# VectorE in place of GpSimd for the low parts of 24 weight units in the mixer of a one-core encoder block

## The chip, the cores and the metric

One core of a Trainium2 chip runs the whole kernel. The metric is the time of one execution on the device in microseconds. Engines are named as in the profile: PE is TensorE, DVE is VectorE, ACT is ScalarE, POOL is GpSimd, SP is SyncE.

## What is computed

One layer of a streaming encoder, on 512 tokens of width 1024, in float32:

```python
x = x + 0.5 * swiglu(rmsnorm(x, ffn1_norm), ffn1_w_gu, ffn1_w_down)
x = x + token_mixing(rmsnorm(x, mix_norm), w_in, lb, hg_norm, conv_w, conv_norm, w_out)
x = x + cross_attention(rmsnorm(x, xa_norm), rmsnorm(mem, mem_norm), xa_wq, xa_wkv, xa_wo)
x = x + 0.5 * swiglu(rmsnorm(x, ffn2_norm), ffn2_w_gu, ffn2_w_down)
return rmsnorm(x, final_norm)
```

`token_mixing` projects the normed x with one matrix (`w_in`, 1024 x 3584) to q, f, i (called v in the kernel) and g of a gated linear recurrence with 4 heads, and to B, C and u of a short convolution with 512 channels. The recurrence's state has a decay exp(cumsum(log f)); its output is normed and multiplied with silu(g). The convolution gives B * conv3(C * u), normed. Both halves together go through `w_out`.

## The kernel before, in words

**Products in three passes.** Every large product takes both of its operands apart into a high part (fp32r, a rounded copy) and a low part (the difference), and adds three matmuls: high x high, high x low, low x high. Lines L1642, L1643 and L1644 are these three.

**Weight units.** The weights lie in HBM as units of 128 x 1024 floats, in the order in which they are used. A unit goes through four steps in one of four slots of the buffers `raw`, `wh` and `wl` (`SLOTS = 4`): SP loads it into `raw` (L492); ACT makes the high part into `wh` (`hi`, L565, counted by the semaphore `hi_ready`); then the low part `wl = raw - wh` is made, counted by `lo_ready`; PE waits for `lo_ready` and multiplies (24 matmuls of 128x512 for a unit), and counts `unit_used`. ACT may make the high part of unit u + 4 only when unit u is used, so it does that in `ahead(u)`. SP reloads `raw` after `lo_ready` of the unit that lay there.

**Who makes the low part.** In parts of the two FFNs DVE does, in one instruction (`unit_low`, L1110). Everywhere else, the mixer included, GpSimd does, in four instructions of 128x256 (`lo`, L531, called from a loop over groups of four units, `whole`).

**The mixer.** The mixer's input projection uses 28 units, `U_MIX` to `U_WOUT` - 1, one in each of 28 slots of the program (the list `MIX_SLOTS`; these slots of time are not the four of the buffers). Slot `at` has a kind ("f", "q", "v", "g", "C", "u", "B") and a number of head or channel group. In slot `at`:
- PE multiplies unit `U_MIX + at` into one of four banks of PSUM (`bank`), after `group_read` says that DVE has read what was there four groups ago, and then does the matmuls of the head steps that the list `STEPS` puts there;
- DVE waits for the unit (`unit_used`), takes it out of the bank, and does its part of the head steps;
- ACT does its part, and `ahead(U_MIX + at)`: the high part of the unit four slots later. In ACT's order it stands behind the head steps O and L with a > 0 of the same slot, and ahead of the others.

The head steps are written out by hand. Head h begins in slot `HEAD_START[h]` = 1, 7, 12, 17 and takes a step in each slot: A (scan of the log decays), L0, L1, L2 (levels of the chunk's triangle), K, Q, S, O, N. In step L, DVE makes differences of b (L1352, L1353), ACT takes their exponentials (L818), DVE multiplies them with q and k (`factors`, L1362), PE makes scores of them (L1894) after the next unit, and DVE keeps the scores under a mask (L1372). L1 stands in slots 3, 9, 14 and 19, and its last DVE instructions are differences (of level 6). L2 stands in slots 4, 10, 15 and 20; in it DVE makes one more difference (L1410), and ACT takes two exponentials of it and of b (L837, L838). K (L1415) follows, then Q, with a transposition that DVE copies out (L1419), and S (L1429, L1431).

Slots 2 to 5 are the four units of v. They fill all four banks at once (four token tiles), and DVE takes them out in slot 5 with four instructions (L1521). PE's unit of slot 6, in the words of the prediction unit 6, uses the first of these banks again. `taps` (L1470 to L1475) makes a convolution after its u slot, and `normed` (L1442 to L1450) the output of a head. L1000 adds squares for a norm.

Of the kernel before, what the change touches and what calls it, by code (L numbers as in the profile page):

```python
# [34 lines left out]
SLOTS = 4  # L35
# [9 lines left out]
U_FFN1 = 0  # L45
# [3 lines left out]
U_MIX = U_DOWN1 + N_DOWN  # L49

MIX_SLOTS = [("f", 0), ("q", 0), ("v", 0), ("v", 1), ("v", 2), ("v", 3),
# [3 lines left out]
V_SLOT = MIX_SLOTS.index(("v", 3)) + 1  # L55
U_WOUT = U_MIX + len(MIX_SLOTS)
# [12 lines left out]
U_FFN2 = U_WO + KC  # L69
# [8 lines left out]
P_UNIT = 2 * NF  # L78
# [28 lines left out]
def block_kernel(nc, w_all, x_t, mem_t, params, consts_mask, ident_d, out):  # L107
    f32 = mybir.dt.float32
# [5 lines left out]
    MULT, ADD, SUB = ALU.mult, ALU.add, ALU.subtract  # L114

    ctx = ExitStack()
    with ctx:
        def sb(name, shape, dt=f32, where=ctx):
            return where.enter_context(nc.sbuf_tensor(name, shape, dt))

        def sem(name):
            return ctx.enter_context(nc.semaphore(name))


        raw = sb("raw", [128, SLOTS, UNIT])
        wh = sb("wh", [128, SLOTS, UNIT], f32r)
        wl = sb("wl", [128, SLOTS, UNIT], f32r)
# [83 lines left out]
        def by_chunk(ap):  # L211

            return ap.rearrange("p (g c t) -> p g c t", g=2, c=2)

        def mirrored(ap):

            *outer, (step, n) = [list(d) for d in ap.ap]
            return bass.AP(ap.tensor, ap.offset + step * (n - 1), outer + [[-step, n]])
# [108 lines left out]
        hi_ready = sem("hi_ready")  # L327
        lo_ready = sem("lo_ready")
# [197 lines left out]
        @block.gpsimd  # L526
        def _(pool):
            def lo(slot):
                for k in range(0, KC, 2):
                    two = slice(128 * k, 128 * k + 256)  # L530
                    ins = nc.gpsimd.tensor_tensor(wl[:, slot, two], raw[:, slot, two], wh[:, slot, two].bitcast(f32), SUB)  # L531
                ins.then_inc(lo_ready, 1)

            def whole(first, last):
                with pool.Fori(first // SLOTS, last // SLOTS) as i:
                    for c in range(SLOTS):
                        pool.wait_ge(hi_ready, i * SLOTS + (c + 1))
                        lo(c)

            def add_up(u0, which, j):  # L540

                p = j % 2
                u = u0 + 2 * (PRE[which] + j) + 1
                pool.wait_ge(raw_loaded[u % SLOTS], u // SLOTS * 16)
                pool.dma_start(raw[:, 2 * p + 1, :], w_all[u, :, :], accum_op=ADD).then_inc(up_added[p], 16)  # L545

            def pairs(u0, which):
                for j in range(ST[which]):
                    add_up(u0, which, j)
                pool.wait_ge(lo_ready, u0 + P_UNIT)  # L550

            pairs(U_FFN1, 0)
            whole(U_FFN1 + P_UNIT, U_FFN2 + SLOTS)
            pairs(U_FFN2, 1)
            whole(U_FFN2 + P_UNIT, NU)

# [394 lines left out]
        def _(dve):  # L951
            steps = [0]

            def link(ins):

                steps[0] += 1
                ins.then_inc(dve_step, 1)
                dve.wait_ge(dve_step, steps[0])
                return ins

            V_ = nc.vector
# [34 lines left out]
            def add_squares(n, off=0):  # L996
                dve.wait_ge(sq_ready, off + (n + 1))
                if n > 0:
                    dve.wait_ge(sq_added, off + n)
                V_.tensor_tensor(acc[:, :], acc[:, :], sq[:, n % 2, :], ADD).then_inc(sq_added, 1)  # L1000
# [9 lines left out]
            def clear():  # L1010

                cleared[0] += 1
                V_.memset(acc[:, :], 0.0).then_inc(acc_clear, 1)
                dve.wait_ge(acc_clear, cleared[0])
# [452 lines left out]
            def taps(at, c):  # L1467
# [6 lines left out]
                                             in1=convV, op0=MULT, op1=ADD))  # L1474
                link(V_.tensor_tensor(convV, convV, rstd[:, :], MULT))  # L1475

            rstd_twice = gbuf[:, 1, :]
            link(V_.tensor_tensor(rstd_twice, rstd[:, :], rstd[:, :], MULT))
            for at, (kind, c) in enumerate(MIX_SLOTS):
                g = SLOT_GROUP[at]  # L1480
                src = bank[g % 4][:, :]
                for st in STEPS[at]:
                    if st[0] == "S":
                        step(*st)
                silu_late = kind == "g" or kind == "q" and ("L", c, 0) not in STEPS[at]
                if kind in "qfg":
                    dve.wait_ge(unit_used, U_MIX + at + 1)
                    if kind == "q" and c >= 2:
                        dve.wait_ge(o_done, c - 1)
                    if kind == "g":  # L1490
                        dst = gb[:, c % 2, :]
                        V_.scalar_tensor_tensor(out=dst, in0=src, scalar=0.5, in1=rstd[:, :], op0=MULT, op1=MULT)\
                            .then_inc(group_read, 1)
                    else:
                        for p in range(2):
                            dst = (q_of if kind == "q" else f_of)(c)[:, :, p, :]
                            last = V_.scalar_tensor_tensor(out=dst if p else mirrored(dst), in0=by_chunk(src)[:, :, p, :],
                                                           scalar=0.5 if kind == "q" else 1.0,
                                                           in1=by_chunk(rstd[:, :])[:, :, p, :], op0=MULT, op1=MULT)
                        last.then_inc(group_read, 1)  # L1500
                    if at == 1:
                        step("A", 0, 0)
                    if not silu_late and kind == "q":
                        silu(kind, c)
                elif kind == "B":
                    dve.wait_ge(unit_used, U_MIX + at + 1)
                    V_.tensor_tensor(convO[:, c, :], src, convV, MULT).then_inc(group_read, 1)
                elif kind == "C":
                    dve.wait_ge(unit_used, U_MIX + at + 1)
                    V_.tensor_tensor(convC, src, rstd_twice, MULT).then_inc(group_read, 1)  # L1510
                elif kind == "u":
                    dve.wait_ge(unit_used, U_MIX + at + 1)
                    dve.wait_ge(group_read, g + 4)
                    V_.tensor_tensor(convU[:, 2:], src, convC, MULT).then_inc(group_read, 1)
                elif c == 0:
                    dve.wait_ge(rms_ready, R["mixcol"] + 1)
                    clear()
                elif c == 3:
                    dve.wait_ge(unit_used, U_MIX + at + 1)
                    for t in range(TT):  # L1520
                        V_.tensor_scalar(V[:, t, :], bank[(G_V + t) % 4][:, :], cols[:, t:t + 1], None, MULT)\  # L1521
                            .then_inc(group_read, 1)
                if at == V_SLOT:
                    dve.wait_ge(v_turned, 1)
                    V_.tensor_copy(V[:, 0, :], o_bank[:, :]).then_inc(v_ready, 1)
                for st in STEPS[at]:
                    if st[0] != "S" and st != ("A", 0, 0):
                        step(*st)
                if at == V_SLOT:
                    dve.wait_ge(v_turned, 2)  # L1530
                    V_.tensor_copy(V[:, 2, :], o_bank[:, :]).then_inc(v_ready, 1)
                if silu_late:
                    silu(kind, c)
                if kind == "u" and MIX_SLOTS[at + 1] == ("B", c):
                    taps(at, c)
                for h in NORMED[at]:
                    normed(h)
                if at and MIX_SLOTS[at - 1][0] == "u" and kind != "B":
                    taps(at - 1, MIX_SLOTS[at - 1][1])
                if kind == "B":  # L1540
                    add_squares(Q_CONV + c)
            dve.wait_ge(rms_ready, R["conv"] + 1)
            for c in range(CC + 1):
                if c < CC:
# [30 lines left out]
            for kind, i in XA_ORDER + [("T", 3), ("O", 3)]:  # L1575
                if kind == "q":
# [4 lines left out]
                    slot = (i // 2) % 2  # L1581
# [601 lines left out]
```

## Time and profile before

| | |
|---|---|
| median of 3 runs | 1094.02 us (1093.92 to 1094.51) |
| the profiled execution | 1094.52 us |
| its span, first to last instruction | 1092.7 us |
| busy in the span: PE, PE's weight loads | 1080.1, 957.9 us |
| busy: DVE, ACT, POOL | 638.7, 527.1, 442.9 us |
| granted clock of TensorE, mean | 0.999 |
| L531, POOL's low parts | 512 instructions, mean 847 ns |

The execution's time is 1.8 us above its span, for what lies around it. Busy time is the union of an engine's instructions. The matmuls' ends are modelled: consecutive matmuls of 128x512 are shown with some 390 ns each, though they begin about 0.23 us apart. A gap in PE's row is therefore shorter than what PE lost. The mixer's slots lie between about 350 and 545 us.

### The profile page before, as it was taken

How to read it: one execution, taken by the hardware profiler on the slowest of the kernel's cores; microseconds unless marked ns; L12 is line 12 of the kernel's file. 1: busy time of each engine (PE TensorE's matmuls, PEld its weight loads, DVE VectorE, ACT ScalarE, POOL GpSimd, SP SyncE). 2: the span in 40 equal slices, each digit the busy share in tenths (PEclk: the TensorE clock that was granted, in tenths of full speed). 3: DMA queues.
4: the chain of work that ended last, by engine and by line, in shares of the span. 5: the costliest groups of instructions: out<-in, count | busy, mean ns of one | idle time of the engine just before them, and what ended most of it. 6: DMA issues, size and time to landing. Idle time of an engine off the chain costs nothing.

```text
span 1092.7 us, 17701 instructions
## 1 busy us (share of the span) xinstructions
PE 1080.1 (99%) x6520; PEld 957.9 (88%) x6520; DVE 638.7 (58%) x944; ACT 527.1 (48%) x739; POOL 442.9 (41%) x546
## 2 busy tenths in 40 slices
PE   9999999999999999999999999999999999999997
PEld 7889999988888888788789888888899999988886
DVE  7887777582223668988477134465977777531002
ACT  6445555542323656564467343354555555633231
POOL 0010000486665444456458874173000000586550
PEclk9999999999999999999999999999999999999999
DMA  7277775332322222122323442122677665333212
GB/s 246 78 206 200 200 202 173 117 114 98 116 96 100 74 84 71 58 97 78 121 73 132 159 152 78 40 86 76 176 203 191 184 184 171 117 117 115 97 58 78
DMA packets 49459, 136.91 MB, mean 125 GB/s; under 512 B 4736, under 2 KB 11008, under 8 KB 49280
## 3 DMA queue, kind: packets, MB, share of 16 engines
q1 hardware_dynamic: 43888, 118.90, 31.1%
q0 software_dynamic: 4320, 15.73, 8.5%
q10 hardware_dynamic: 1200, 1.57, 0.4%
q8 instruction: 35, 0.57, 0.2%
q14 instruction: 16, 0.13, 0.0%
HBM read 134.09 MB, written 2.10 MB: 125 GB/s over the span
## 4 chain that ended last, share of the span: by engine, by line
PE 52%; POOL 25%; issue 21%; DVE 1%; POOLq 0%; DMA 0%; ACT 0%; DVEq 0%; SPq 0%; ACTq 0%
POOL wl L531 25%; PE bank L1642 8%; PE bank L1644 8%; PE bank L1643 8%; PE bank L1757 4%; PE bank L1756 4%; PE bank L1755 4%; PE score L1757 3%; PE score L1756 3%; PE score L1755 3%; PE bank L1653 2%; PE o_bank L1757 1%; PE o_bank L1756 1%; PE o_bank L1755 1%; PE bank L1711 1%
## 5 line engine op out<-in xcount | busy, mean ns | idle before, releaser
L531 POOL TENSOR_TENSOR wl<-raw,wh 128x256 fp32r<-128x256 f32 x512 | 416.6, 847 | 306.4 <-ACT wh L565 263.7
L565 ACT ACTIVATE wh<-raw 128x1024 fp32r<-128x1024 f32 x120 | 125.8, 1053 | 126.0 <-PE bank L1644 119.4
L1642 PE MATMUL bank<-xh,wh 128*128 128x512 f32 x392 | 157.7, 402 | 0.6 <-DVE V L1521 0.6
L545 POOL DMA_DIRECT2D raw<-w_all x30 | 26.1, 869 | 318.0 <-DMA raw<-w_all 318.0
L1644 PE MATMUL bank<-xh,wl 128*128 128x512 f32 x392 | 153.2, 391 | 0.0
L1643 PE MATMUL bank<-xl,wh 128*128 128x512 f32 x392 | 153.1, 390 | 0.0
L1642 PE MATMUL bank<-zr,wh 128*128 128x512 f32 (+1 forms) x374 | 141.0, 377 | 0.0
L1644 PE MATMUL bank<-zr,wl 128*128 128x512 f32 (+1 forms) x374 | 140.8, 377 | 0.0
L1643 PE MATMUL bank<-zr,wh 128*128 128x512 f32 (+1 forms) x374 | 140.8, 377 | 0.0
L1020 DVE SCALAR_TENSOR_TENSOR x<-bank,x 128x512 f32<-128x512 f32 (+1 forms) x31 | 21.3, 686 | 160.4 <-PE bank L1644 160.1
L578 ACT ACTIVATE wh<-raw 128x1024 fp32r<-128x1024 f32 x50 | 52.9, 1058 | 86.6 <-PE bank L1644 53.8
L1642 PEld LDWEIGHTS bank<-xh,wh 128*128 128x128 f32 x392 | 73.6, 188 | 17.6 <-issue 2.5
L1643 PEld LDWEIGHTS bank<-xl,wh 128*128 128x128 f32 x392 | 73.6, 188 | 16.8 <-issue 1.9
L1110 DVE TENSOR_TENSOR wl<-raw,wh 128x1024 fp32r<-128x1024 f32 x72 | 87.5, 1217 | 1.3 <-ACT wh L578 0.8
L1644 PEld LDWEIGHTS bank<-xh,wl 128*128 128x128 f32 x392 | 73.5, 188 | 16.0
L1643 PEld LDWEIGHTS bank<-zr,wh 128*128 128x128 f32 x374 | 70.4, 188 | 12.9
L1644 PEld LDWEIGHTS bank<-zr,wl 128*128 128x128 f32 x374 | 70.4, 188 | 12.9
L1642 PEld LDWEIGHTS bank<-zr,wh 128*128 128x128 f32 x374 | 70.4, 188 | 12.8
L1642 PE MATMUL bank<-cat_h,wh 128*128 128x512 f32 x128 | 50.6, 395 | 0.5 <-POOL wl L531 0.5
L1643 PE MATMUL bank<-cat_l,wh 128*128 128x512 f32 x128 | 49.8, 389 | 0.0
L1644 PE MATMUL bank<-cat_h,wl 128*128 128x512 f32 x128 | 49.8, 389 | 0.0
L1000 DVE TENSOR_TENSOR acc<-acc,sq 128x512 f32<-128x512 f32 x43 | 42.5, 989 | 10.1 <-ACT sq L600 6.6
(331 smaller groups left out, 2687.4 us busy)
## 6 DMA issues: line engine op xcount, KB each, us to landing
raw<-w_all SPq DMA_DIRECT2D x200, 512.0 KB, 3.3
raw<-w_all POOLq DMA_DIRECT2D x30, 512.0 KB, 5.2
zf<-w_all SPq DMA_DIRECT2D x30, 256.0 KB, 4.4
x<-x_t SPq DMA_DIRECT2D x8, 256.0 KB, 6.0
out_t<-x SPq DMA_DIRECT2D x8, 256.0 KB, 2.4
raw<-w_all SPq DMA_DIRECT2D x6, 256.0 KB, 6.1
memf<-mem_t ACTq DMA_DIRECT2D x1, 1024.0 KB, 4.7
raw<-w_all ACTq DMA_DIRECT2D x2, 256.0 KB, 4.1
```

What stands on the lines that cost most here:

```text
L531: ins = nc.gpsimd.tensor_tensor(wl[:, slot, two], raw[:, slot, two], wh[:, slot, two].bitcast(f32), SUB)
L545: pool.dma_start(raw[:, 2 * p + 1, :], w_all[u, :, :], accum_op=ADD).then_inc(up_added[p], 16)
L565: nc.scalar.activation(wh[:, slot, :], raw[:, slot, :], ACT.Copy).then_inc(hi_ready, 1)
L578: nc.scalar.activation(wh[:, slot, :], raw[:, slot, :], ACT.Copy).then_inc(hi_ready, 1)
L1000: V_.tensor_tensor(acc[:, :], acc[:, :], sq[:, n % 2, :], ADD).then_inc(sq_added, 1)
L1110: V_.tensor_tensor(wl[:, slot, :], raw[:, slot, :], wh[:, slot, :].bitcast(f32), SUB).then_inc(lo_ready, 1)
L1642: nc.tensor.matmul(out_, a[0], b_[0], start=first, stop=False)
L1643: nc.tensor.matmul(out_, a[0], b_[1], start=False, stop=False)
L1644: return nc.tensor.matmul(out_, a[1], b_[0], start=False, stop=last)
L1755: nc.tensor.matmul(out_, a[0][:, ks], bh, start=first and k == 0, stop=False, skip_group_check=True)
L1756: nc.tensor.matmul(out_, a[0][:, ks], bl, start=False, stop=False, skip_group_check=True)
L1757: last = nc.tensor.matmul(out_, a[1][:, ks], bh, start=False, stop=k == 3, skip_group_check=True)
```

## The change

POOL's loop is cut in two. It makes the low parts up to the mixer's first four units, waits until `lo_ready` has counted all of the mixer's units, and goes on with `U_WOUT`. Between them, DVE makes the low parts of the other 24: at the end of slot `at`, for `at` from 0 to 23, that of unit `U_MIX + at + 4`, in one instruction. It waits for `lo_ready` (all earlier units) and for `hi_ready` of its own unit. Nothing else is changed.

```diff
--- before.py
+++ after.py
@@ -550,7 +550,9 @@
                 pool.wait_ge(lo_ready, u0 + P_UNIT)
 
             pairs(U_FFN1, 0)
-            whole(U_FFN1 + P_UNIT, U_FFN2 + SLOTS)
+            whole(U_FFN1 + P_UNIT, U_MIX + SLOTS)
+            pool.wait_ge(lo_ready, U_WOUT)
+            whole(U_WOUT, U_FFN2 + SLOTS)
             pairs(U_FFN2, 1)
             whole(U_FFN2 + P_UNIT, NU)
 
@@ -1474,6 +1476,13 @@
                                              in1=convV, op0=MULT, op1=ADD))
                 link(V_.tensor_tensor(convV, convV, rstd[:, :], MULT))
 
+            def weight_low(u):
+
+                slot = u % SLOTS
+                dve.wait_ge(lo_ready, u)
+                dve.wait_ge(hi_ready, u + 1)
+                V_.tensor_tensor(wl[:, slot, :], raw[:, slot, :], wh[:, slot, :].bitcast(f32), SUB).then_inc(lo_ready, 1)
+
             rstd_twice = gbuf[:, 1, :]
             link(V_.tensor_tensor(rstd_twice, rstd[:, :], rstd[:, :], MULT))
             for at, (kind, c) in enumerate(MIX_SLOTS):
@@ -1539,6 +1548,8 @@
                     taps(at - 1, MIX_SLOTS[at - 1][1])
                 if kind == "B":
                     add_squares(Q_CONV + c)
+                if at + SLOTS < len(MIX_SLOTS):
+                    weight_low(U_MIX + at + SLOTS)
             dve.wait_ge(rms_ready, R["conv"] + 1)
             for c in range(CC + 1):
                 if c < CC:
```

In the changed kernel, lines behind the first edit have numbers that are 2 higher, and those behind the second 9 higher; the new instruction is L1484.

The first place that the prediction speaks of is DVE at the end of slot 3, in slot 4 and at the start of slot 5. Before (L1353 is the end of slot 3's differences, L1410 the end of slot 4, L1521 the copies of V that begin slot 5):

```order
L1352 TENSOR_TENSOR X<-b 128x256
L1353 TENSOR_TENSOR X<-b 128x256
L1352 TENSOR_TENSOR X<-b 128x64x4
L1353 TENSOR_TENSOR X<-b 128x64x4
...
L1362 TENSOR_TENSOR X<-X,qf 128x256x2
L1410 TENSOR_TENSOR both<-b 128x2x256
L1521 TENSOR_SCALAR V<-bank,cols 128x512 x4
```

And now:

```order
L1354 TENSOR_TENSOR X<-b 128x256
L1355 TENSOR_TENSOR X<-b 128x256
L1484 TENSOR_TENSOR wl<-raw,wh 128x1024
L1354 TENSOR_TENSOR X<-b 128x64x4
L1355 TENSOR_TENSOR X<-b 128x64x4
...
L1364 TENSOR_TENSOR X<-X,qf 128x256x2
L1412 TENSOR_TENSOR both<-b 128x2x256
L1484 TENSOR_TENSOR wl<-raw,wh 128x1024
L1530 TENSOR_SCALAR V<-bank,cols 128x512 x4
```

A low part stands behind the last differences of slot 3, and another between L1410 (now L1412) and the copies of V.

The second place is DVE from the end of slot 15 into slot 17: L1458 ends slot 15, L1497 to L1450 are slot 16, L1510 begins slot 17. Before:

```order
L1410 TENSOR_TENSOR both<-b 128x2x256
L1458 SCALAR_TENSOR_TENSOR gb<-gbuf,gb 128x512
L1497 SCALAR_TENSOR_TENSOR qf<-bank,rstd 128x2x128 x2
L1372 COPY_PREDICATED tri<-masks,score 128x256 x2
L1415 TENSOR_TENSOR both<-both,qf 128x4x128
L1463 SCALAR_TENSOR_TENSOR qf<-gbuf,qf 128x2x128 x2
L1442 TENSOR_TENSOR onrm<-o_bank,osq 128x2x128 x2
L1447 SCALAR_TENSOR_TENSOR onrm<-onrm,par,gb 128x512
L1450 TENSOR_TENSOR cat_l<-onrm,cat_h 128x512
L1510 TENSOR_TENSOR ubuf<-bank,gbuf 128x512
```

And now:

```order
L1412 TENSOR_TENSOR both<-b 128x2x256
L1460 SCALAR_TENSOR_TENSOR gb<-gbuf,gb 128x512
L1484 TENSOR_TENSOR wl<-raw,wh 128x1024
L1506 SCALAR_TENSOR_TENSOR qf<-bank,rstd 128x2x128 x2
L1374 COPY_PREDICATED tri<-masks,score 128x256 x2
L1417 TENSOR_TENSOR both<-both,qf 128x4x128
...
L1452 TENSOR_TENSOR cat_l<-onrm,cat_h 128x512
L1484 TENSOR_TENSOR wl<-raw,wh 128x1024
L1519 TENSOR_TENSOR ubuf<-bank,gbuf 128x512
```

Each slot now ends with a low part; the rest of the order is as it was, on DVE, ACT, PE and SP.

## Rows read from the trace of the kernel before

**Rows 1.** The page, busy time of each engine (share of the span) and instructions

```profile
PE 1080.1 (99%) x6520; PEld 957.9 (88%) x6520; DVE 638.7 (58%) x944; ACT 527.1 (48%) x739; POOL 442.9 (41%) x546
```

**Rows 2.** The page, the chain that ended last, by engine and line

```profile
POOL wl L531 25%; PE bank L1642 8%; PE bank L1644 8%; PE bank L1643 8%; PE bank L1757 4%; PE bank L1756 4%; PE bank L1755 4%; PE score L1757 3%; PE score L1756 3%; PE score L1755 3%; PE bank L1653 2%; PE o_bank L1757 1%; PE o_bank L1756 1%; PE o_bank L1755 1%; PE bank L1711 1%
```

**Rows 3.** Timeline of PE, slot 6: start, us, engine, line, operation [idle <-releaser]

```profile
386.00 0.47 PE L1642 MATMUL bank<-xh,wh 128*128 128x512 f32 x1 [0.61 <-DVE V L1521]
386.30 0.39 PE L1643 MATMUL bank<-xl,wh 128*128 128x512 f32 x1
386.53 0.40 PE L1644 MATMUL bank<-xh,wl 128*128 128x512 f32 x1
```

**Rows 4.** Timeline of PE, slot 13 and behind the mixer

```profile
441.36 0.49 PE L1918 MATMUL n_bank<-V,kdT 128*128 128x128 f32 x3
...
450.75 1.16 PE L1894 MATMUL score<-X 128*128 128x128 f32 x6 [1.52 <-DVE X L1362]
...
543.48 1.12 PE L1693 MATMUL n_bank<-acc,ones 128*128 128x512 f32 x2 [0.61 <-DVE acc L1000]
```

**Rows 5.** The page, costliest groups: xcount, busy us, mean ns, idle before

```profile
L531 POOL TENSOR_TENSOR wl<-raw,wh 128x256 fp32r<-128x256 f32 x512 | 416.6, 847 | 306.4 <-ACT wh L565 263.7
...
L1110 DVE TENSOR_TENSOR wl<-raw,wh 128x1024 fp32r<-128x1024 f32 x72 | 87.5, 1217 | 1.3 <-ACT wh L578 0.8
```

**Rows 6.** Windows, slots 10 to 21: length, PE PEld DVE ACT POOL, PEclk, DMA

```profile
421.30:510.90 89.60, 88.08 (x456) 74.81 (x456) 78.08 (x134) 55.91 (x74) 45.93 (x52) 1.00 0.20 71
```

**Rows 7.** DVE by form, 421.3:510.9: xcount, busy us, mean ns, idle

```profile
L1362 DVE TENSOR_TENSOR X<-X,qf 128x512 f32<-128x512 f32 x17 | 13.7, 846 | 1.1 <-ACT X L818 1.0
L1353 DVE TENSOR_TENSOR X<-b 128x256 f32<-128x256 f32 x16 | 8.3, 519 | 0.0
```

**Rows 8.** Timeline of DVE, ends of slots 9, 14 and 15

```profile
417.56 0.68 DVE L1362 TENSOR_TENSOR X<-X,qf 128x512 f32<-128x512 f32 x1
...
457.45 0.42 DVE L1353 TENSOR_TENSOR X<-b 128x256 f32<-128x256 f32 x1
...
464.86 0.66 DVE L1458 SCALAR_TENSOR_TENSOR gb<-gbuf,gb 128x512 f32<-128x512 f32 x1
```

**Rows 9.** Timeline of DVE, slots 4 and 5

```profile
378.56 0.43 DVE L1352 TENSOR_TENSOR X<-b 128x256 f32<-128x256 f32 x1 [0.35 <-PE score L1894]
...
380.81 3.87 DVE L1362 TENSOR_TENSOR X<-X,qf 128x512 f32<-128x512 f32 x3
...
385.12 2.68 DVE L1521 TENSOR_SCALAR V<-bank,cols 128x512 f32<-128x512 f32 x4
```

**Rows 10.** Timeline of ACT, slots 3 to 5

```profile
378.82 1.05 ACT L565 ACTIVATE wh<-raw 128x1024 fp32r<-128x1024 f32 x1
...
385.23 0.63 ACT L837 ACTIVATE both<-both 128x512 f32<-128x512 f32 x1 [4.27 <-DVE both L1410]
...
386.29 1.99 ACT L565 ACTIVATE wh<-raw 128x1024 fp32r<-128x1024 f32 x2
```

**Rows 11.** Timeline of DVE, slots 13, 16, 21 and 22

```profile
446.10 0.28 DVE L1429 COPY S<-n_bank 128x128 f32<-128x128 f32 x1
...
471.71 0.76 DVE L1463 SCALAR_TENSOR_TENSOR qf<-gbuf,qf 128x256 f32<-128x256 f32 x2 [4.04 <-ACT gbuf L862]
...
506.44 0.76 DVE L1442 TENSOR_TENSOR onrm<-o_bank,osq 128x256 f32<-128x256 f32 x2 [2.16 <-ACT osq L616]
...
510.90 0.68 DVE L1510 TENSOR_TENSOR ubuf<-bank,gbuf 128x512 f32<-128x512 f32 x1
```

**Rows 12.** Timeline of ACT, high parts of slots 14 and 15

```profile
458.48 1.05 ACT L565 ACTIVATE wh<-raw 128x1024 fp32r<-128x1024 f32 x1
...
466.03 1.04 ACT L565 ACTIVATE wh<-raw 128x1024 fp32r<-128x1024 f32 x1
```

**Rows 13.** Timeline of PE, scores behind unit 22

```profile
506.18 0.82 PE L1894 MATMUL score<-X 128*128 128x128 f32 x4
```

## The prediction, made before the changed kernel was run

> **What bounds the kernel.** The page comes first: TensorE (PE) is busy for 1080.1 us, 99% of the span [rows 1]. The ends of matmuls are modelled there, so the share alone proves little; its idle rows say more. The chain of waits gives 25% to GpSimd's low parts, L531 [rows 2], which reads as if GpSimd were the bound. But PE's timeline is nearly gapless, and where it does stop in the mixer, VectorE (DVE) releases it: 0.61 us before the first matmul of unit 6, released by the copy of V (L1521) [rows 3]; 1.52 us in slot 13, released by DVE's L1362; and 0.61 us behind the mixer, released by L1000 [rows 4]. So in the mixer PE is the bound, DVE stands close behind it, and GpSimd has room. These three make 2.7 us; that is the most that the change can win. What it can lose is read from DVE's own work.
>
> The profiled execution took 1094.52 us against a median of 1094.02; my sum gives a difference, which I add to the median.
>
> **Removed.** GpSimd made a low part in four subtractions of 128x256 [rows 5]. For 24 units, 96 of them go. They were on no path that ends anything: GpSimd is busy for 45.93 of 89.60 us in slots 10 to 21 [rows 6]. Their direct value is nothing. Their indirect value is that DVE is slowed while they run: in the same stretch L1362 means 846 ns and L1353 519 ns [rows 7], against 0.68 and 0.42 us where GpSimd rests [rows 8]. Summed over all groups of the stretch, mean less shortest times count, I get 12.0 us; L1362 is the largest with 17 x 0.17 = 2.9, L1353 gives 16 x 0.10 = 1.6, and the rest is made of groups of 2 to 16 alike. The ends for this relief are 0 (if something else slows them) and 12.0; I take 12.0, since I found the long cases inside GpSimd's spans and the short ones outside.
>
> **Added.** 24 subtractions of 128x1024 on DVE. The same form exists in the FFN: L1110, 1217 ns [rows 5]. An instruction begins some 0.08 us before the one ahead ends, so each takes 1.14 us of the queue. The wait for `lo_ready` asks for earlier units and is met. The wait for `hi_ready` is another matter: the high part of the unit four ahead is made by ScalarE (ACT) in the same slot, behind ACT's work for the head's steps. Where the slot holds step L with a = 1 or 2, ACT first takes exponentials of DVE's last differences. Queued behind the waiting DVE instruction is all of the next slot; PE waits for that work.
>
> **Place 1, slots 4 and 5.** Before, DVE began slot 4 at 378.56, finished its three L1362 (3.87 us) and L1410, and began the copies of V at 385.12 [rows 9]. ACT then made two exponentials from 385.23 and, of the two high parts that begin at 386.29, the first, which with 1.05 us ends at 387.34 [rows 10]; nobody on DVE waited for it. Now:
> - Slot 3's high part ended at 378.82 + 1.05 = 379.87 [rows 10]. The relief makes it earlier by 0 to 2 us; I take 1.2. With 1.2 us for the low part slot 4 begins at 379.85, 1.3 late.
> - The three L1362 need 1.9 us in place of 3.87, so slot 4's work ends at 385.20 + 1.3 - 1.95 = 384.55.
> - The high part ends 2.1 us later, at 386.65, the low part at 387.9, and the first copy of V (0.73 us) at 388.6, against 385.85.
> PE's unit 6 needs that bank, and did wait for it [rows 3]. So PE loses **2.75 us**, with nothing to hide it: its idle time grows from 0.6 to 3.4 us. In slots 6 to 8 DVE waits for PE ahead of its next slot by more than a low part takes, so those hide.
>
> **Place 2, slots 10 to 13.** Three low parts (3.4 us) and 0.45 us after slot 9 stand against some 6 us of relief. DVE reaches slot 13 earlier relative to PE, and the stall of 1.52 us goes: **-1.5 us** [rows 4].
>
> **Place 3, slots 10 to 22.** Here DVE runs without a gap between slots; what it must do in addition reaches PE sooner or later. Count to the start of slot 22, at 510.90 before [rows 11]:
> - shift of place 1: +2.75, and +0.45 since slot 9's high part comes after DVE is done;
> - 12 low parts of 1.14: +13.7;
> - waits for `hi_ready`: in slot 14 DVE ended at 457.45 + 0.42 = 457.87 and the high part at 458.48 + 1.05 = 459.53, so 1.65; in slot 15 465.52 and 467.07, so 1.55; slot 20 is built as slot 15 and gets the same [rows 8, 12]. +4.75;
> - relief: -12.0;
> - DVE already idled in this stretch for ACT, 4.04 us in slot 16 and 2.16 in slot 21 [rows 11]. Those waits hang on ACT's chain behind the very high parts of slots 15 and 20, so the wait and the low part fall into them: 2.7 and 2.16 are absorbed, -4.9.
> DVE starts slot 22 at 510.90 + 4.75 = 515.65. Before, PE had finished slot 22 at about 506.3, when the scores behind it begin at 506.18 [rows 13], 4.6 us ahead of DVE. Slot 13 shows the limit of such a lead: PE was done at 441.36, DVE began at 446.10, 4.7 us behind, and PE then stood still [rows 4, 11]. With the same lead PE finishes slot 22 at 511.05, **4.8 us** late, in which places 1 and 2 are contained: 2.75 - 1.5 + 3.55. If PE could lead by a whole slot (64.8 us over 9 units, 7.2) it would be 2.2; if only by 4.7 - 1.5 = 3.2, 6.2. From slot 24 on nothing is added, DVE catches up, and the lost time is not returned, as PE is the bound to the end.
>
> Sum: 1094.0 + 4.8 = **1098.8 us**.
>
> One rule bears on the relief. The Trainium skill (Perfetto Trace Analysis, Optimizing Scalar/DVE Operations) notes that GpSimd and VectorE share a read port of SBUF, so that moving work between them might not help. By it the sum would be about nothing. The rows agree with the sharing (519 ns in the mean against 0.42 us), but they price the two sides apart, which the rule does not.
>
> **Rivals.**
> *Nothing measurable* (within 0.2%). DVE's 12.0 us of relief and its idle times pay for the low parts, and place 1 shrinks to the size of the stalls that vanish: 2.75 - 1.5 = 1.25, at 1095.3. For it: busy time nearly balances, 13.7 against 12.0 in the gapless stretch. Against: the waits for `hi_ready` are not busy time. This is what the skill's sentence would give. 0.15.
> *Faster.* If ACT's high parts came before DVE needs them everywhere, places 1 and 3 would be free, and the stalls of 2.7 us would go: 1091.3. It decides by whether slot 4's high part is done before 385.2; its row says 387.34 [rows 10]. 0.08.
> *The clock falls.* In this trace the granted clock is 1.00 of full speed over the whole stretch, the 1.52 us stall included [rows 6]; no row shows a stop of 3.4 us as place 1 makes one. If it fell to the lower level (1.2 instead of 2.4 GHz) for one unit of 24 matmuls, which begin 0.23 us apart [rows 3], their 5.5 us would be 11, and the sum 1104.3. The Trainium skill (TensorE: Matmul & The Clock Gate, Part 1 on the HAM clock gate) says that an idle array drops to that level and rises again with activity; the trace neither shows nor excludes it. 0.07.
> *The relief fails.* If DVE isn't sped up, place 3 alone grows by up to 12 us: 1110.8. 0.04.
>
> **Numbers.** A measurement of this kernel can tell about 0.2% (2.2 us) from no change. My forecast (slower by 2.2 to 6.2 us) has 0.66; with the two slow rivals, slower has 0.77. Same 0.15, faster 0.08. The range goes down to 1094.5, which leaves out the faster case and half of the same case, and up to 1104.0, above the forecast's own end at 1100.2 by the uncertainty of the relief; what is left out is about 0.2.
>
> **What would show it.** PE's first matmul of unit 6 waits over 2.5 us for V; the stall in slot 13 is gone; DVE's low parts in slots 3, 4, 9, 14, 15, 20 start just when ACT's high part ends; L1362 means some 0.68 us in the mixer; and from slot 15 to 22 PE waits often, for under 1.5 us each, on DVE's L1362, L1415, L1419. I am wrong if PE has no more idle time after slot 14 than before, or if unit 6 starts as promptly as it did.

## The result, and the profile after

| | before | changed |
|---|---|---|
| median, us | 1094.21 (1093.92 to 1094.51, 4 runs) | 1102.11 (1101.19 to 1103.32, 4 runs) |
| profiled execution, its span | 1094.52, 1092.7 | 1101.86, 1100.0 |
| mean granted clock | 0.999 | 0.996 |

The ratio is 1.0072 [1.006, 1.0083]: the change makes the kernel slower by 7.9 us. The forecast was 1098.8 with a range of 1094.5 to 1104.0. The sign and the range hold; the forecast is 3.3 us short. The two profiled executions differ by 7.3 us, and the rest of this section places those.

The page of the changed kernel, its busy times, the granted clock in 40 slices, the chain by engine, and the costliest GpSimd group:

```profile
PE 1085.1 (99%) x6520; PEld 960.4 (87%) x6520; DVE 646.0 (59%) x968; ACT 527.4 (48%) x739; POOL 359.1 (33%) x450
...
PEclk9999999999999989999999999999999999999999
...
PE 36%; POOL 9%; issue 6%; DVE 1%; ACT 0%; POOLq 0%; DVEq 0%
...
L531 POOL TENSOR_TENSOR wl<-raw,wh 128x256 fp32r<-128x256 f32 x416 | 332.9, 834 | 397.6 <-ACT wh L567 355.2
```

Against [rows 1, 2], GpSimd lost 84 us of busy time and most of its share of the chain, and the kernel got slower: that share was indeed no sign of a bound. DVE has 24 instructions more but only 7.3 us more of busy time, where the low parts alone are 27 (24 x 1.14 of the queue): DVE's other work got shorter by some 20 us. This is the relief of the prediction, and it is real. And one slice of the clock shows an 8 where before all showed 9. It is the 15th, 385.0 to 412.5 us, where unit 6 begins.

PE's timeline there and further on (start, us, engine, line, operation, idle before and who ended it):

```profile
384.15 1.09 PE L1905 MATMUL score<-X 128*128 128x128 f32 x8
389.14 0.77 PE L1653 MATMUL bank<-xh,wh 128*128 128x512 f32 x1 [3.90 <-DVE V L1530]
389.70 0.63 PE L1654 MATMUL bank<-xl,wh 128*128 128x512 f32 x1
390.13 0.63 PE L1655 MATMUL bank<-xh,wl 128*128 128x512 f32 x1
...
394.39 0.47 PE L1653 MATMUL bank<-xh,wh 128*128 128x512 f32 x1
394.70 0.40 PE L1654 MATMUL bank<-xl,wh 128*128 128x512 f32 x1
394.94 0.39 PE L1655 MATMUL bank<-xh,wl 128*128 128x512 f32 x1
...
484.28 0.91 PE L1929 MATMUL n_bank<-V,kdT 128*128 128x128 f32 x6 [0.89 <-DVE kdT L1421]
...
506.82 0.99 PE L1905 MATMUL score<-X 128*128 128x128 f32 x5 [0.43 <-DVE X L1364]
```

Unit 6 waits 3.90 us for the copies of V, where it waited 0.61 [rows 3]. Then its first matmuls begin 0.43 us apart instead of 0.23 and are shown with 0.63 us each instead of 0.39. At 394.39 they are short again. The windows say why (length; PE, PEld, DVE, ACT, POOL; clock; DMA):

```profile
384.00:387.70 3.70, 1.24 (x10) 0.98 (x8) 1.47 (x3) 2.79 (x4) 0.00 (x0) 1.00 0.00 0
387.70:394.50 6.80, 5.36 (x13) 4.24 (x14) 5.77 (x9) 1.53 (x2) 0.00 (x0) 0.50 0.23 77
394.50:397.30 2.80, 2.80 (x14) 2.32 (x13) 0.00 (x0) 0.00 (x0) 0.00 (x0) 0.99 0.53 187
421.30:510.90 89.60, 88.11 (x442) 72.95 (x441) 77.29 (x144) 53.89 (x71) 0.00 (x0) 1.00 0.20 69
```

The granted clock is 0.50 of full speed (1.2 in place of 2.4 GHz) from 387.7, when PE had stood still for over 2 us, to 394.5, more than 5 us after it had resumed. Twelve matmuls at 0.43 instead of 0.23 us are 2.4 us; with what lies around them the unit loses 2.6 us beyond its wait.

How DVE came to be late is in its timeline: the end of slot 3 to slot 5, and then the ends of slots 14 and 15 and DVE's wait in slot 16:

```profile
378.67 1.22 DVE L1484 TENSOR_TENSOR wl<-raw,wh 128x1024 fp32r<-128x1024 f32 x1 [1.74 <-ACT wh L567]
379.81 0.42 DVE L1354 TENSOR_TENSOR X<-b 128x256 f32<-128x256 f32 x1
...
382.05 2.30 DVE L1364 TENSOR_TENSOR X<-X,qf 128x512 f32<-128x512 f32 x3
384.19 0.68 DVE L1412 TENSOR_TENSOR both<-b 128x512 f32<-128x512 f32 x1
387.10 1.23 DVE L1484 TENSOR_TENSOR wl<-raw,wh 128x1024 fp32r<-128x1024 f32 x1 [2.23 <-ACT wh L567]
388.25 2.72 DVE L1530 TENSOR_SCALAR V<-bank,cols 128x512 f32<-128x512 f32 x4
...
464.30 1.23 DVE L1484 TENSOR_TENSOR wl<-raw,wh 128x1024 fp32r<-128x1024 f32 x1 [1.75 <-ACT wh L567]
...
473.32 1.22 DVE L1484 TENSOR_TENSOR wl<-raw,wh 128x1024 fp32r<-128x1024 f32 x1 [1.64 <-ACT wh L567]
...
477.86 0.76 DVE L1465 SCALAR_TENSOR_TENSOR qf<-gbuf,qf 128x256 f32<-128x256 f32 x2 [1.17 <-ACT gbuf L864]
```

The low part of slot 4 waits 2.23 us for ACT, since ACT first takes two exponentials, one of what L1412 has just made and one of b:

```profile
384.90 0.63 ACT L839 ACTIVATE both<-both 128x512 f32<-128x512 f32 x1 [2.96 <-DVE both L1412]
385.44 0.61 ACT L840 ACTIVATE both<-b 128x512 f32<-128x512 f32 x1
385.96 1.99 ACT L567 ACTIVATE wh<-raw 128x1024 fp32r<-128x1024 f32 x2
```

It is PE's banks that stand behind that waiting instruction: the copies of V, which free them, begin at 388.25 instead of 385.12 [rows 9]. In slot 16 DVE's own wait for ACT has shrunk from 4.04 to 1.17 us [rows 11]: the low part in front of it filled it.

The relief, by form, in the window of [rows 7], 421.3 to 510.9 us (count, busy us, mean ns, idle before):

```profile
L1364 DVE TENSOR_TENSOR X<-X,qf 128x512 f32<-128x512 f32 x19 | 13.5, 751 | 1.1 <-ACT X L820 1.0
L1484 DVE TENSOR_TENSOR wl<-raw,wh 128x1024 fp32r<-128x1024 f32 x11 | 13.4, 1222 | 5.2 <-ACT wh L567 5.1
L1355 DVE TENSOR_TENSOR X<-b 128x256 f32<-128x256 f32 x18 | 7.5, 419 | 0.0
```

L1355 is back at 419 ns (from 519), L1364 at 751 (from 846) [rows 7]; some of its forms are longer than 0.68 us with GpSimd at rest. The window doesn't hold the same work in both traces, since DVE comes 6 to 8 us later to each slot in the changed kernel (19 of L1364 stand in it against 17). Taken in order, instruction by instruction, DVE's 134 instructions of slots 10 to 21 add up to 86.3 us before and to 74.5 us now: 11.8 us of relief.

Where PE lost its time against the execution of before, read from the moment at which it counts each unit as used:

| place | lost, us |
|---|---|
| slots 4 to 6: the longer wait of unit 6 | +3.3 |
| slots 4 to 6: the low clock behind it | +2.6 |
| slots 7 to 14 | 0 |
| the stall of 1.52 us at 450.75 [rows 4], gone | -1.98 |
| slots 16 to 23, in seven steps of 0.1 to 1.1 | +3.67 |
| slot 24 on | 0 |
| start of the run | -0.23 |

The sum, 7.4, is the difference of the two executions (7.3). Of the seven steps five are 0.45 us or more. At these the trace names DVE as the releaser of PE's weight loads, L1364 four times and L1421 once; the other two are 0.1 each.

### The profile page after: what moved, and what is told of

It reads as the page before. It is cut to its first block, busy times and chain, and to the rows that moved or that the text cites. A ratio compares the mean times of both kernels' runs of the same rounds, so it can differ in the third digit from the quotient of the medians.

```text
span 1100.0 us, 17581 instructions
## 1 busy us (share of the span) xinstructions
PE 1085.1 (99%) x6520; PEld 960.4 (87%) x6520; DVE 646.0 (59%) x968; ACT 527.4 (48%) x739; POOL 359.1 (33%) x450
## 4 chain that ended last, share of the span: by engine, by line
PE 36%; POOL 9%; issue 6%; DVE 1%; ACT 0%; POOLq 0%; DVEq 0%
POOL wl L531 9%; PE bank L1653 6%; PE bank L1654 6%; PE bank L1655 6%; PE bank L1767 2%; PE bank L1768 2%; PE bank L1766 2%; PE bank L1664 2%; PE score L1767 2%; PE score L1768 2%; PE score L1766 2%; PE o_bank L1767 1%; PE o_bank L1768 1%; PE o_bank L1766 1%; DVE wl L1484 0%
## 5 line engine op out<-in xcount | busy, mean ns | idle before, releaser
L531 POOL TENSOR_TENSOR wl<-raw,wh 128x256 fp32r<-128x256 f32 x416 | 332.9, 834 | 397.6 <-ACT wh L567 355.2
L1128 DVE TENSOR_TENSOR zr<-sq,zr 128x1024 fp32r<-128x1024 f32 x30 | 36.8, 1225 | 18.6 <-ACT zr L671 18.6
```

The lines of the kernel that those rows point to most:

```text
L1128: V_.tensor_tensor(sum_l, sums, sum_h.bitcast(f32), SUB).then_inc(sums_lo, 1)
```

## Experiments

The first four share their runs of before (1094.47, 27 runs), the last four likewise (1094.09, 27 runs). Their edits are against the changed kernel unless said otherwise.

The theory had two parts by now: an instruction that waits for ACT stands in DVE's queue ahead of work that PE needs (places 1 and 3), and the stop that this makes lowers the clock. The rivals were that DVE's added busy time is what costs, wherever it stands, and that the clock is a chance of the run.

**The low part at the end of slot 4 goes into slot 5, behind the copies of V.** (By the program's count it belongs to `at` = V_SLOT - 2.)

```diff
+                    weight_low(U_MIX + at - 1 + SLOTS)
...
-                if at + SLOTS < len(MIX_SLOTS):
+                if at + SLOTS < len(MIX_SLOTS) and at != V_SLOT - 2:
```

> Slot 4's low part is made behind the copies of V at the start of slot 5 instead of ahead of them; all else is as in the change. Theory (the waits that the low parts stand for in DVE's order cost the time, and the low clock is only a consequence of PE's stop): unit 6 starts within 1 us of the scores before it, the granted clock never falls, slot 6 no longer loses its 5.8 us, so about 1096.3 us. Slots 16 to 23 keep their loss of 3.7 us. Rival (DVE has too much to do, wherever it is put): the wait moves to the next slots and the time stays above 1100.

Measured: 1096.13 (1095.74 to 1097.57, 11 runs), ratio 1.0017 [1.0008, 1.0026]. PE's unit 6, and DVE in slot 5:

```profile
385.83 0.47 PE L1654 MATMUL bank<-xh,wh 128*128 128x512 f32 x1 [0.43 <-DVE V L1530]
```

```profile
384.95 2.71 DVE L1530 TENSOR_SCALAR V<-bank,cols 128x512 f32<-128x512 f32 x4
387.58 1.21 DVE L1484 TENSOR_TENSOR wl<-raw,wh 128x1024 fp32r<-128x1024 f32 x1
```

Taken between the two medians, the place of one instruction out of 24 is worth 6.0 us of the 7.9. The work is the same, only PE's banks come free ahead of it. Unit 6 waits 0.43 us and no stretch of low clock follows. Slots 16 to 23 lose 3.69 us as before, the stall at 450.75 is gone as before.

**Every low part one slot later**, when its high part is long there.

```diff
-                if at + SLOTS < len(MIX_SLOTS):
-                    weight_low(U_MIX + at + SLOTS)
+                if at > 0 and at + SLOTS - 1 < len(MIX_SLOTS):
+                    weight_low(U_MIX + at + SLOTS - 1)
```

> Each of the 24 low parts is made one slot later, so that its high part was made in the slot before; DVE's work is the same. Theory (waiting for the high part is what is lost in slots 14, 15, 19, 20, not the 1.2 us of work): the waits for hi_ready are gone, V is copied in time, no clock fall, the stall of slot 13 stays away: 1092 to 1093.5 us, so a little faster than before the change. Rival (the added work itself costs slots 16 to 23 their 3.7 us): 1096 us, since only slot 6 is repaired.

Measured: 1093.51 (1093.15 to 1094.3, 11 runs), ratio 0.9991 [0.9982, 1.0]. DVE by form, slots 10 to 21:

```profile
L1484 DVE TENSOR_TENSOR wl<-raw,wh 128x1024 fp32r<-128x1024 f32 x12 | 14.7, 1221 | 0.1
```

The same busy time, and 0.1 us of idle time ahead of it in place of 5.2. That takes 8.6 us off the changed kernel, so DVE's added work isn't what made it slow. PE's unit 6, and its scores ahead of unit 22:

```profile
386.13 0.47 PE L1653 MATMUL bank<-xh,wh 128*128 128x512 f32 x1 [0.18 <-DVE V L1530]
...
499.00 0.71 PE L1905 MATMUL score<-X 128*128 128x128 f32 x4 [0.43 <-DVE X L1364]
```

Unit 6 waits 0.18 us and costs nothing. What the work itself costs is 1.26 us in slots 16 to 23, in two steps: 0.41 ahead of unit 20 and 0.85 ahead of unit 22, of which the second row shows the wait. The kernel stands within the 0.2% that can't be told from no change. I had expected 1092 to 1093.5, with no loss named for the work.

**The relief alone.** Against the kernel before: GpSimd subtracts 16 of 1024 columns of those 24 units, and nobody the rest; the low parts are left out of the result.

```diff
+            def touch(first, last):
+                with pool.Fori(first // SLOTS, last // SLOTS) as i:
+                    for c in range(SLOTS):
+                        pool.wait_ge(hi_ready, i * SLOTS + (c + 1))
+                        nc.gpsimd.tensor_tensor(wl[:, c, 0:16], raw[:, c, 0:16], wh[:, c, 0:16].bitcast(f32), SUB)\
+                            .then_inc(lo_ready, 1)
...
-            whole(U_FFN1 + P_UNIT, U_FFN2 + SLOTS)
+            whole(U_FFN1 + P_UNIT, U_MIX + SLOTS)
+            touch(U_MIX + SLOTS, U_WOUT)
+            whole(U_WOUT, U_FFN2 + SLOTS)
```

> From the kernel before: GpSimd only subtracts 16 of 1024 columns of each of the 24 units, nobody makes the rest of the low parts (left out of the computation). This is the relief alone. Theory (GpSimd slows DVE's two-input instructions): L1362 means about 0.68 us in place of 0.85 in slots 10 to 21, PE's stall of 1.5 us in slot 13 goes and that before unit 6 shrinks, so about 1091.7 us. Rival (something else slows DVE): 1094.2 and unchanged means.

Measured: 1092.0 (1091.86 to 1093.21, 11 runs), ratio 0.9979 [0.997, 0.9988]. DVE by form, slots 10 to 21 (L1371 and L1362 are here what L1364 and L1355 are above):

```profile
L1371 DVE TENSOR_TENSOR X<-X,qf 128x512 f32<-128x512 f32 x17 | 12.2, 762 | 0.1
L1362 DVE TENSOR_TENSOR X<-b 128x256 f32<-128x256 f32 x16 | 6.7, 419 | 0.0
```

DVE's times fall with GpSimd's absence alone, as they do in the changed kernel, though L1364's form stops at 762 ns and not at the 0.68 us expected. All that PE wins by it is 2.6 us, 1.98 in the stall at 450.75 and 0.58 at unit 6.

**PE kept busy while unit 6 waits.** Fourteen matmuls into a bank that nothing reads then, ahead of the unit:

```diff
+                    if at == V_SLOT:
+                        for _ in range(14):
+                            nc.tensor.matmul(o_bank[:, :], xh[:, 0, 0:128], xh[:, 1, :], start=True, stop=True)
                     group(u, SLOT_GROUP[at], x_phase=1 if at == 0 else None)
```

> The change, with 14 matmuls of 128x512 added on PE into a free bank ahead of unit 6, where it waits for V (3.2 us of them inside a wait of 3.9). Theory (the clock fell since PE stood still there): the granted clock stays at 1.00, unit 6 starts at the same 389.1 and its matmuls are 0.23 us apart, so 2.6 us less than the change: 1099.5 us. Rival (the clock falls for another reason, or the time isn't lost there): 1102 us.

Measured: 1099.63 (1099.48 to 1099.73, 5 runs), ratio 1.0047 [1.0033, 1.006], clock 0.999. PE's timeline:

```profile
384.33 1.09 PE L1905 MATMUL score<-X 128*128 128x128 f32 x8
385.16 3.43 PE L1976 MATMUL o_bank<-xh 128*128 128x512 f32 x14
389.34 0.47 PE L1653 MATMUL bank<-xh,wh 128*128 128x512 f32 x1 [0.75 <-DVE V L1530]
389.64 0.40 PE L1654 MATMUL bank<-xl,wh 128*128 128x512 f32 x1
389.88 0.39 PE L1655 MATMUL bank<-xh,wl 128*128 128x512 f32 x1
```

Unit 6 begins at 389.34, no earlier than in the changed kernel (389.14), but its matmuls begin 0.24 to 0.30 us apart from the first. Slots 4 to 6 lose 3.38 us where they lost 5.90. So the low clock follows from PE's standing still, and costs 2.5 us in itself. The runs of this kernel also lie within 0.25 us, those of the changed one within 2.1: there the mean clock of a run goes from 0.996 (1101.19, 1101.86) to 0.994 (1102.35, 1103.32). That fits a low clock whose length differs from run to run and costs more than 2.6 us in the median, but only one of these runs has a trace, so it is not shown.

**GpSimd works beside DVE.** DVE makes the low parts as in the change, and GpSimd does as much as before, four subtractions of 128x256 for each of the 24 units, into a tile that is free then.

```diff
+        pool_step = sem("pool_step")
...
+            for u in range(U_MIX + SLOTS, U_WOUT):
+                pool.wait_ge(hi_ready, u + 1)
+                pool.wait_ge(pool_step, u - U_MIX - SLOTS)
+                for k in range(4):
+                    to = cat_h[:, KC - 2 + k // 2, 256 * (k % 2):256 * (k % 2) + 256]
+                    ins = nc.gpsimd.tensor_tensor(to, x[:, k, 0:256], x[:, k, 256:512], SUB)
+                ins.then_inc(pool_step, 1)
             pool.wait_ge(lo_ready, U_WOUT)
```

> The change, and in addition GpSimd does four subtractions of 128x256 for each of the 24 units, at the same moments as before the change, on other data into a place that nobody reads. So DVE has the added work and not the relief. Theory (the relief is real and worth 12 us of DVE's time in slots 10 to 21): L1362 means some 0.85 us again, the stall of slot 13 comes back or grows, and slots 15 to 23 lose 6 to 14 us more than in the change: 1108 to 1116 us. Rival (GpSimd's work never mattered): 1102 us.

Measured: 1124.54 (1124.26 to 1125.2, 4 runs), ratio 1.0279 [1.0263, 1.0295]: far above what I expected (1108 to 1116). DVE by form over the mixer (L1492 is the low part, L1372 the L1364 of above), then PE's unit 6, then windows in the columns of above:

```profile
L1492 DVE TENSOR_TENSOR wl<-raw,wh 128x1024 fp32r<-128x1024 f32 x24 | 39.9, 1662 | 13.1 <-ACT wh L575 12.9
...
L1372 DVE TENSOR_TENSOR X<-X,qf 128x512 f32<-128x512 f32 x28 | 21.4, 806 | 1.7 <-ACT X L828 1.6
```

```profile
396.26 0.76 PE L1661 MATMUL bank<-xh,wh 128*128 128x512 f32 x1 [5.55 <-DVE V L1538]
```

```profile
390.63:400.80 10.17, 4.62 (x12) 3.60 (x12) 7.83 (x11) 4.33 (x5) 7.01 (x8) 0.50 0.17 52
484.00:490.00 6.00, 4.63 (x17) 3.88 (x18) 4.25 (x8) 3.04 (x5) 0.34 (x1) 0.72 0.00 1
```

I had counted only the lost relief. But the new instruction is itself slowed, from 1222 to 1662 ns, 10.6 us over the 24, on top of what the relief was worth, and each stop of PE grows: slots 4 to 6 lose 12.6 us, slots 12 to 15 5.8, slots 16 to 23 10.1 and slot 24 1.6. With as much work left on GpSimd, DVE's low parts cost 30 us; freed of it, they cost 8.

**The first 16 units, then the first 12**, each one slot later as in the second experiment; GpSimd makes the rest. The edit for 16; for 12, each 20 is a 16:

```diff
-            pool.wait_ge(lo_ready, U_WOUT)
-            whole(U_WOUT, U_FFN2 + SLOTS)
+            pool.wait_ge(lo_ready, U_MIX + 20)
+            whole(U_MIX + 20, U_FFN2 + SLOTS)
...
+                if at > 0 and at + SLOTS - 1 < 20:
+                    weight_low(U_MIX + at + SLOTS - 1)
```

> DVE makes the low parts of the 16 units U_MIX+4 to U_MIX+19, each one slot later than in the change (slots 1 to 16); GpSimd makes the last 8 as before the change. Theory (DVE has room up to slot 16, and in slots 17 to 24 GpSimd's work costs less than DVE's own): the stall in slot 13 is gone, that before unit 6 is smaller by 0.4, and the losses of slots 20 and 22 (1.26 us in the run one slot later) are gone: 1092.1 us, faster than before the change by 2.3. Rival (GpSimd's work in slots 16 to 23 slows DVE until PE waits): 1093.5 or more.

> As e6, but DVE makes 12 (U_MIX+4 to U_MIX+15, slots 1 to 12) and GpSimd the last 12. Theory: GpSimd works from slot 12 on, which brings back part of DVE's delay at slot 13: between 1092.1 and 1094.0 us. Rival (slots 10 and 11 alone decide the stall): the same as e6.

Sixteen: 1095.3 (1094.25 to 1096.43, 11 runs), ratio 1.001 [1.0001, 1.0019]; the expectation was 3 us too good, and what came is its rival. PE and DVE in the slot where GpSimd begins again:

```profile
485.76 0.71 PE L1905 MATMUL score<-X 128*128 128x128 f32 x4 [2.00 <-DVE X L1364]
```

```profile
483.63 0.94 DVE L1355 TENSOR_TENSOR X<-b 128x256 f32<-128x256 f32 x1
484.50 1.81 DVE L1364 TENSOR_TENSOR X<-X,qf 128x512 f32<-128x512 f32 x2
```

The second experiment has its wait of 0.41 us in this same slot: PE's lead over DVE is just used up there by the low parts. GpSimd's return makes 0.42 us of L1355 into 0.94, and PE stands still for 2.00 us. Twelve: 1094.39 (1094.14 to 1094.96, 11 runs), ratio 1.0002 [0.9993, 1.0011], no different from before, and 0.4 us above the range expected. The stall of slot 13, which the relief takes away elsewhere, is back (0.93 us here, and 0.42 ahead of the next scores of the slot):

```profile
450.13 0.71 PE L1905 MATMUL score<-X 128*128 128x128 f32 x4 [0.93 <-DVE X L1364]
```

A split gives DVE the work in one part and takes the relief away in the other. The runs of the sixteen differ by 2.2 us; their mean clock is 0.999 at 1094.3 and 0.997 at 1095.7 and above. The profiled one is among the quick ones and shows no low clock behind its stop of 2.00 us. The others may have one there, but no trace shows it, and the mean clock alone doesn't prove it: the kernel before has a run with 0.997 at 1094.0.

**The waits alone.** The new instruction takes 16 of 1024 columns; the rest of the low parts is left out.

```diff
-                V_.tensor_tensor(wl[:, slot, :], raw[:, slot, :], wh[:, slot, :].bitcast(f32), SUB).then_inc(lo_ready, 1)
+                V_.tensor_tensor(wl[:, slot, 0:16], raw[:, slot, 0:16], wh[:, slot, 0:16].bitcast(f32), SUB).then_inc(lo_ready, 1)
```

> The change with DVE's low parts cut to 16 of 1024 columns (the rest of these 24 low parts is left out of the computation): DVE waits for the high part as in the change, with hardly any work. Theory (in place 3 the waits alone are covered, and so nearly is the work alone, only both together reach PE): unit 6 starts at about 386.3, no clock fall, slots 16 to 23 lose under 0.5 us, 1093 us. Rival (the waits alone are what slots 16 to 23 lose): 3 us more there, 1096 us.

Measured: 1093.38 (1092.89 to 1094.09, 11 runs), ratio 0.9993 [0.9984, 1.0002].

```profile
L1484 DVE TENSOR_TENSOR wl<-raw,wh 128x16 fp32r<-128x16 f32 x14 | 2.4, 172 | 6.9 <-ACT wh L567 6.8
```

The waits are all there, 6.9 us of idle time, but behind slot 14 they cost PE nothing, and at unit 6 only 0.84 us against before. With the three kernels together, PE's loss in slots 16 to 23 is: waits alone 0, work alone 1.26, both 3.67. So they don't add. It fits one lead of PE over DVE on which both draw, so that only what exceeds it arrives.

## Why the prediction came out as it did

**What bounds the kernel: right.** PE's idle rows, not GpSimd's 25% of the chain, told what could be won; the relief alone wins 2.5 us at most, where the text had 2.7. In PE's own terms it won 1.98 at the second stall, which had been read as 1.52, and 0.58 at the first; the third (L1000) stayed.

**Removed, and the relief: right.** I took 12.0 us for slots 10 to 21; the same 134 instructions now take 11.8 us less. L1355 came to the 0.42 us named, L1364 to 0.75, not to 0.68. The Trainium skill (SBUF — State Buffer, section "SBUF: two separate sides") says that a VectorE operation with two inputs in SBUF and a GpSimd operation that reads SBUF hold one pair of ports in turn, for a whole instruction. The trace agrees that such operations are longer beside GpSimd (519 against 419 ns, 1662 against 1222), while one with an input in PSUM is not (L1497, now L1506: 413 and 416 ns). The outcome of "about nothing" from the rule on moving work between the two did not come. It is near, though, where the waits are gone: one slot later, the same work stands against the same relief, and the kernel is within 0.2% of before.

**Added: right.** 1.2 us each, 1222 ns in the mean. They wait for ACT in the six slots named, 1.64 to 2.23 us each. They also do so in slot 0 (1.86 us), which was not named and cost PE nothing.

**Place 1: right in mechanism, 0.5 short in size.** The timeline against the working: slot 4 begins at 379.81 (379.85), its work ends at 384.87 (384.55), the low part at 388.33 (387.9), the first copy of V at 388.98 (388.6). PE's extra wait is 3.3 us against 2.75. Most of the 0.5 is the three L1364, which take 2.30 us and not 1.9.

**Place 2: right.** -1.98 against -1.5.

**Place 3: right.** +3.67 against +3.55. DVE begins slot 10 at 427.47 in place of 421.34, which is 6.1 us late: 3.3 of place 1, 2.6 of the low clock and 0.5 less a start of the run that was 0.2 earlier, where I had 3.2 without the clock. To the start of slot 22 the terms are then 13.7 for the low parts (13.7), 5.0 for the waits of slots 14, 15 and 20 (4.75), -11.8 for the relief (-12.0) and -5.0 for what fell into DVE's own waits for ACT (-4.9). DVE starts slot 22 (L1519) at 518.95; less the 2.6 us of the low clock that is 516.35, against 515.65. The pattern of several waits under 1.5 us each came as named, on L1364 and L1421; L1417 ended none. The working added waits and work; the last experiment shows that this holds only once PE's lead is used up, as it was here.

**The term that the sum lacked** is the low clock. The sum was made of places 1 to 3, with nothing to hide place 1 and nothing behind it either. The low clock was kept apart as a rival with 0.07, on the ground that the trace showed the clock at 1.00 through a stall of 1.52 us and no stop of 3.4. It came, beside the forecast and not in place of it: 3.3 - 1.98 + 3.67 is 5.0 against the 4.8 of the sum, and 2.6 us (2.5 by the kernel with PE kept busy) is what the sum lacked. The rival's own price was twice too high: I had all 24 matmuls of the unit at half speed, 5.5 us, and it was 12 of them. The Trainium skill (TensorE: Matmul & The Clock Gate, Part 1) says that an idle array drops to 1.2 GHz. The trace agrees, with a granted clock of 0.50 from 387.7 on; read as a rule for this change it deserved more than 0.07, as the predicted stop was more than twice as long as any that the trace had excused.

That the result lies in the range is in part luck. It is above 1100.2, the forecast's own end. The range went on to 1104.0 for the uncertainty of the relief, and the relief came as forecast; what filled that room was the clock.

What remains of the difference in medians (7.9 against 7.3 of the profiled executions) may be the clock too, as the slower runs have the lower mean clock; no trace shows it.

## What to carry to other kernels

Before an instruction that waits for another engine is put into an in-order queue, read what stands directly behind it there and who needs that: here one of 24 places held PE's banks back and made 6.0 of the 7.9 us, and moving it by one step was enough. Where a change makes TensorE stand still longer than any stop in the trace of before, price the clock as a term of the sum, not as a remote rival; here it was a third of the loss. And an engine that is freed is worth what its neighbour is relieved of: take that from long and short cases of one form, and expect it back wherever the freed engine works again.

## What the runs showed that was not expected

- The low clock outlasts the stop that caused it by far: PE resumed at 389.14 and had its full clock at 394.5. A stop of 3.9 us cost 2.6 us more.
- The length of a stop doesn't decide it alone. Before's 1.52 us [rows 4, 6] and the 2.00 us in the kernel with sixteen units were followed by none in their profiled executions; in the kernel with GpSimd beside, the clock is 0.72 in the mean of 484.0 to 490.0, around a stop of 1.67 us (second row). The same kernel has a low clock from 390.63 on, when its stop of 5.55 us had hardly begun (390.7): what lies ahead is a stop of 2.49 us (first row) and 1.4 us of scores.

```profile
389.36 1.35 PE L1913 MATMUL score<-X 128*128 128x128 f32 x8 [2.49 <-DVE X L1372]
...
485.37 1.66 PE L1913 MATMUL score<-X 128*128 128x128 f32 x8 [1.67 <-DVE X L1372]
```

- Fourteen matmuls without use, in time that was lost anyway, gave back 2.5 us.
- Beside GpSimd the instruction of 1024 columns goes from 1222 to 1662 ns, 36% more, where the forms of L1353 and L1362 had been 24% and 13% longer beside it (519 against 419, 846 against 751). GpSimd's own subtractions are longer too, 1071 ns in the mean against 905 between 356 and 560 us of before. Both engines wait for the same high part there and then start together, which may be why; no run separates it.
